# First modulation of a two-block transformer kernel computed in two column halves, with four tiles of the first chunk pair placed between the second half's products

## What is computed

```python
c_act = jax.nn.silu(c)
mod = (c_act @ w_ada[l] + b_ada[l]).reshape(B, N_SUBLAYERS, N_MOD, D_MODEL)
u = modulate(rmsnorm(h, norm1_g[l]), mod[:, 0, 0], mod[:, 0, 1])   # x * (1 + scale) + shift
h = h + FFN_RES_WEIGHT * mod[:, 0, 2][:, None, :] * swiglu(u, ffn1_w_gu[l], ffn1_w_down[l])
```

## Time and profile before

| | us |
|---|---|
| median of 3 runs | 2110.93 |
| the profiled execution | 2111.26 |
| its span | 2109.5 |
| PE busy in the span | 2085.0 (99%) |
| DVE busy | 1295.6 (61%) |
| ACT busy | 879.7 (42%) |
| POOL busy | 349.0 (17%) |

### The profile page before, as it was taken

How to read it: one execution, slowest core, us unless ns; L and a number is a source line. 1 busy time by engine, 2 the same in 40 slices (tenths; PEclk the granted TensorE clock), 3 DMA queues, 4 the chain that set the end, 5 groups by cost and what they waited for, 6 DMA issues and landing times.

```text
span 2109.5 us, 28671 instructions
## 1 busy us (share of the span) xinstructions
PE 2085.0 (99%) x9520; PEld 1711.7 (81%) x9520; DVE 1295.6 (61%) x1587; ACT 879.7 (42%) x1265; POOL 349.0 (17%) x263
## 2 busy tenths in 40 slices
PE   8999999999999999999999999999999999999998
PEld 5888888888888878888887788888888888888886
DVE  5787567678754553333357867777333577547767
ACT  5322223477543342222245656664222344334444
POOL 2999998000000200000000000022000000000000
PEclk9999999999999999999999999999999999999999
DMA  8666764322233323233323222233333233333232
GB/s 297 186 182 178 206 190 141 107 70 70 72 93 100 105 80 99 81 99 100 92 78 99 74 70 70 63 72 94 107 99 90 80 100 92 94 103 99 69 94 87
DMA packets 372645, 225.82 MB, mean 107 GB/s; under 512 B 8377, under 2 KB 361826, under 8 KB 372592
## 3 DMA queue, kind: packets, MB, share of 16 engines
q1 hardware_dynamic: 362976, 193.49, 31.4%
q0 software_dynamic: 9616, 31.64, 5.4%
HBM read 223.00 MB, written 2.10 MB: 107 GB/s over the span
## 4 chain that ended last, share of the span: by engine, by line
PE 92%; DVE 4%; ACT 2%; issue 1%; DMA 1%; SPq 1%; DVEq 0%; POOL 0%; ACTq 0%
PE ps L495 29%; PE ps L497 29%; PE ps L496 29%; PE ps L639 1%; PE ps L627 1%; PE ps L654 1%; PE ps L628 1%; PE ps L655 1%; DVE wl L1514 0%; PE ps L880 0%; DMA wada<-in_w_ada 0%; SPq L393 0%; DMA xtok<-in_x 0%; PE ps L630 0%; DVE tmp L1564 0%
## 5 line engine op out<-in xcount | busy, mean ns | idle before, releaser
L495 PE MATMUL ps<-uh,wh 128*128 128x512 f32 x1848 | 725.4, 393 | 2.0 <-DVE ul L1570 1.8
L497 PE MATMUL ps<-uh,wl 128*128 128x512 f32 x1848 | 719.9, 390 | 0.0
L496 PE MATMUL ps<-ul,wh 128*128 128x512 f32 x1848 | 719.5, 389 | 0.0
L1514 DVE TENSOR_TENSOR wl<-raw,wh 128x1024 fp32r<-128x1024 f32 x389 | 554.2, 1429 | 202.6 <-ACT wh L1024 196.1
L1024 ACT ACTIVATE wh<-raw 128x1024 fp32r<-128x1024 f32 x389 | 407.2, 1052 | 190.8 <-PE ps L497 187.7
L495 PEld LDWEIGHTS ps<-uh,wh 128*128 128x128 f32 x1848 | 347.0, 188 | 77.0 <-DVE ul L1570 3.4
L497 PEld LDWEIGHTS ps<-uh,wl 128*128 128x128 f32 x1848 | 346.8, 188 | 73.1
L496 PEld LDWEIGHTS ps<-ul,wh 128*128 128x128 f32 x1848 | 347.1, 188 | 71.0 <-issue 0.5
L495 PE MATMUL ps<-ah,wh 128*128 128x512 f32 x528 | 208.9, 396 | 0.0
L496 PE MATMUL ps<-al,wh 128*128 128x512 f32 x528 | 208.8, 396 | 0.0
L497 PE MATMUL ps<-ah,wl 128*128 128x512 f32 x528 | 208.8, 395 | 0.0
(11 more groups left out here) (337 smaller groups left out, 2389.4 us busy)
## 6 DMA issues: line engine op xcount, KB each, us to landing
raw<-in_ffn_w_gu SPq DMA_DIRECT2D x88, 512.0 KB, 4.6
raw<-in_w_in SPq DMA_DIRECT2D x57, 512.0 KB, 3.8
ada_ring<-in_w_ada POOLq DMA_DIRECT2D x56, 512.0 KB, 4.1
raw<-in_w_up SPq DMA_DIRECT2D x44, 512.0 KB, 3.8
raw<-in_w_mix_in SPq DMA_DIRECT2D x40, 512.0 KB, 3.9
raw<-in_ffn_w_down SPq DMA_DIRECT2D x32, 384.0 KB, 3.3
raw<-in_ffn_w_down SPq DMA_DIRECT2D x32, 320.0 KB, 2.9
wada<-in_w_ada SPq DMA_DIRECT2D x16, 512.0 KB, 9.8
```

Of the source, the lines that this page charges most:

```text
L495: pe.matmul(dst, lh, rh, start=first, stop=False, skip_group_check=True)
L496: pe.matmul(dst, lh, rl, start=False, stop=False, skip_group_check=True)
L497: return pe.matmul(dst, ll, rh, start=False, stop=last, skip_group_check=True)
L1514: dve.tensor_tensor(wl[:, w], raw[:, w], wh[:, w].bitcast(F32), ALU.subtract).then_inc(w_lo, 1)
```

## The change

The halves are no longer scale and shift, but the first and the last 512 features of both:

- **Loads.** `load_half(half)` issues eight DMAs of 512 KB; each takes 512 columns of the shift and the same 512 of the scale (two runs of 2 KB per row). Their semaphores and their place among SP's loads stay.
- **PE.** Within a half, PE sums all 512 scale columns and DVE all 512 shift columns. Between the second half's products come tiles 0 to 3 of the first chunk pair (after products 1, 2, 3 and 4), and tiles 4 to 7 after the second `keep_clock(2)`.
- **DVE.** `columns(half)` now ends with the gain of its four tiles. `split(0)`, `shifted_lo(0)` and `split(1)` follow the first half; then `shifted_lo` of tiles 1 to 3 alternates with the second half's sums. `normalise` of tile 3 comes before the last two sums of the first half.
- **ACT** goes tile by tile: gain, then shift; `split(1)` after tile 0 and `split(2)` ahead of tile 4.
- **POOL** normalises tiles 4 to 7, once DVE has done tiles 0 to 3.
- **att2** (DVE only). In the lead-in `split(nb + 2 + LEAD)` moves from before `first_result(3)` to after `v_lo(0)` and `maxima(0, 0)`. In the first body, `o_sum(p, 0)` and `turned_lo(p, 1)` move ahead of `split(nb + 5 + LEAD)`, so also ahead of `f_rows(p)`.
- The waits on `derived` count one more.

```diff
+            def load_half(half):
+
+                by_vector = wada[:, :].rearrange("p (v k c) -> p v k c", v=2, k=DT)
+                for k in range(DT):
+                    w = a["w_ada"][0, k * P:(k + 1) * P, 0:2 * D].rearrange("p (v c) -> p v c", v=2)
+                    sp.dma_start(by_vector[:, :, k, half * S:(half + 1) * S], w[:, :, half * S:(half + 1) * S]).then_inc(HALF_LD[half][k][0], 16)
+
+            load_half(0)
...
+            load_half(1)
...
+            def pair_tile(c, banks, k, kt, xh, xl, ready):
+
+                pe.wait_ge(ready[0], ready[1] + k + 1)
+                x = slice(k * S, (k + 1) * S)
+                for n, b in enumerate(banks):
+                    r = (c + n) % RING
+                    w = slice(r * SLOT + k * P, r * SLOT + (k + 1) * P)
+                    mm = mm3(bank(b), wh[:, w], wl[:, w], xh[:, x], xl[:, x], k == 0, k == kt - 1)
+                    if k == kt - 1:
+                        mm.then_inc(chunk_done, 1)
...
-            column_sums(1, ada_acc[1])
-
-            pe.wait_ge(h_new, 2 + 5)
+            column_sums(0)
+
+            pe.wait_ge(h_new, 2 + DT)
+            nb = AT_["ffn1"]
             for k in range(DT):
-                pe.wait_ge(*SHIFT_LD[k])
-                x = (DT + k) * D
-                mm = pe.matmul(bank(4), cbc[:, k * P:(k + 1) * P], wada[:, x:x + S], start=k == 0, stop=k == DT - 1, skip_group_check=True)
-            mm.then_inc(ada_red, 1)
+                mm = scale_sum(1, k, 4)
+                if k == DT - 1:
+                    mm.then_inc(ada_red, 1)
+                if 1 <= k <= 4:
+                    if k == 1:
+                        pe.wait_ge(w_lo, RING + nb + 2)
+                    pair_tile(nb, (0, 1), k - 1, DT, uh, ul, u_at(0))
             keep_clock(2)
 
             pe.wait_ge(ada0, 1 + 2 * DT)
-            column_sums(0, ada_acc[0])
+            pe.wait_ge(mods_done, 2)
+            column_sums(1)
             keep_clock(2)
+            for k in range(4, DT):
+                pair_tile(nb, (0, 1), k, DT, uh, ul, u_at(0))
...
+            def gained(m):
+
+                act.wait_ge(norm_t, m + 1)
+                act.wait_ge(derived, 1 if m < 4 else 2)
+                act.activation(tile(hn, m), tile(hn, m), ACT.Copy, scale=gains[:, m:m + 1]).then_inc(x_inv, 1)
+
+            def shifted_hi(m):
+
+                act.wait_ge(x_inv, 3 + m + 1)
+                act.wait_ge(mods_done, 2 if m < 4 else 4)
+                act.activation(tile(uh, m), tile(hn, m), ACT.Identity, bias=mods[:, m:m + 1]).then_inc(norm_hi, 1)
+
+            gained(0)
+            shifted_hi(0)
             split(1, 0)
...
+            for m in range(1, DT):
+                if m == 4:
+                    split(2, 0)
+                gained(m)
+                shifted_hi(m)
...
+                    if first:
+                        o_sum(p, 0)
+                        turned_lo(p, 1)
+                    if not last:
                         split(nb + 5 + LEAD, it)
...
-                    split(nb + 2 + LEAD, 0)
                     first_result(3, B_F0)
...
                 if kind == 2:
+                    split(nb + 2 + LEAD, 0)
                     normal(4)
...
+            weighted(0, range(3))
 
             dve.wait_ge(x_inv, 3)
             normalise((0, 1))
-            scale_part((3, 4, 5))
-            normalise((2,))
-            scale_part((6, 7))
+            weighted(0, (3, 4, 5))
+            normalise((2, 3))
+            weighted(0, (6, 7))
...
-            normalise((3,))
-            columns(1, 6, sq, 0)
-            dve.wait_ge(mods_done, 2)
-            gain_of(0, C_N1, 1)
-            normalise((4,))
+            columns(0, 6, sq)
             split(0, 0)
+            shifted_lo(0)
             split(1, 0)
...
+            for m in range(1, 4):
+                shifted_lo(m)
+                weighted(1, (m - 1,))
+            weighted(1, range(3, DT))
+            columns(1, 4, tmp)
+            for m in range(4, 7):
+                shifted_lo(m)
             split(2, 0)
+            shifted_lo(7)
...
+            pool.wait_ge(x_inv, 3)
+            pool.wait_ge(norm_t, 4)
+            for m in range(4, DT):
+                pool.wait_ge(h_new, 2 + m + 1)
+                pool.tensor_tensor(tile(hn, m), tile(h, m), inv[:, :], ALU.mult).then_inc(norm_t, 1)
+
             pool.wait_ge(c_act, 1)
```

More of the change, by code:

```diff
@@ L517, in dense_pair @@
                 for k in range(kt):
[L519 to L526, removed]
+                    pair_tile(c, banks, k, kt, xh, xl, ready)
                     if middle is not None and k == 3:
@@ L1407, in _ @@
             split(0, 0)
-            split(1, 0)
[L1410 to L1420, removed]
+            def gained(m):
[8 more added lines that the diff above has]
+            shifted_hi(0)
+            split(1, 0)
+            for m in range(1, DT):
[3 more added lines that the diff above has]
+                shifted_hi(m)
             ffn("ffn1", False)
@@ L1910, in body @@
                         layer_stats()
-                    o_sum(p, 0)
+                    if not first:
+                        o_sum(p, 0)
                     if kind == 2 and not last:
                         f_rows(p)
-                    turned_lo(p, 1)
+                    if not first:
+                        turned_lo(p, 1)
                     if kind == 2 and not last:
@@ L2036, in _, with weighted @@
             dve.tensor_copy(cbc[:, :].rearrange("p (k n) -> p k n", n=P), cact[:, :].unsqueeze(2).to_broadcast([P, DT, P])).then_inc(ada0, 1)
[L2038 to L2049, removed]
-                for k in ks:
[L2051 to L2057, removed]
+            def weighted(half, ks):
+                acc = ada_acc[0][:, half * S:(half + 1) * S]
+                for k in ks:
+                    dve.wait_ge(*HALF_LD[half][k])
+                    w = ada_half(0, k, half)
+                    if k == 0:
+                        dve.tensor_scalar(acc, w, cact[:, 0:1], None, ALU.mult).then_inc(ada0, 1)
+                    else:
+                        dve.wait_ge(ada0, 1 + DT * half + k)
+                        dve.scalar_tensor_tensor(acc, w, cact[:, k:k + 1], acc, ALU.mult, ALU.add).then_inc(ada0, 1)
             def normalise(ms):
@@ L2076, in columns @@
                 dve.wait_ge(ada_red, 2 * n + 2)
-                dve.tensor_tensor(mods[:, v * DT + half:(v + 1) * DT], bank(7, 400 + 4 * (1 - v), half), cols[:, c + half:c + DT],
+                dve.tensor_tensor(mods[:, n0:n0 + 4], bank(7, 400 + 4 * half, 4), cols[:, C_BADA + n0:C_BADA + n0 + 4],
                                   ALU.add).then_inc(mods_done, 1)
+                dve.wait_ge(mods_done, 2 * n + 1)
+                dve.scalar_tensor_tensor(gains[:, n0:n0 + 4], mods[:, m0:m0 + 4], 1.0, cols[:, C_N1 + n0:C_N1 + n0 + 4],
+                                         ALU.add, ALU.mult).then_inc(derived, 1)
@@ L2080, in _, with shifted_lo @@
+            def shifted_lo(m):
+                dve.wait_ge(norm_hi, m + 1)
+                dve.wait_ge(mods_done, 2 if m < 4 else 4)
+                dve.scalar_tensor_tensor(tile(ul, m), tile(hn, m), mods[:, m:m + 1], tile(uh, m).bitcast(F32), ALU.add, ALU.subtract).then_inc(u_ready, 1)
             dve.wait_ge(rms_done, 1)
             dve.reciprocal(small[:, 8:12], small[:, 4:8]).then_inc(inv_done, 1)
-            scale_part(range(3))
+            weighted(0, range(3))
             dve.wait_ge(x_inv, 3)
```

64 lines of the change are left out of this document (26 added, 38 removed).

## The result

The kernel after takes 2115.23 us (median of 20 runs, 2113.30 to 2117.45), the kernel before beside it 2112.14 (20 runs, 2110.93 to 2113.17): +3.1 us, a ratio of 1.0015 with a 95% interval from 1.0008 to 1.0021. It lies within 0.2%, on the slower side.

A forecast was written before the change was run, and what follows sets the result against it. PE, busy 99% of the span, was taken as the bound. 2111.26 (profiled execution) + 3.0 for the start − 1.4 for att2 = 2112.9, lowered 0.33 to the median: 2112.5 us, range 2109.8 to 2116.0.

The forecast's parts named there:

- Collision of POOL and DVE: Start, ahead of tile 0: POOL's ops hold DVE's two-input ops exclusively, so the gain is done at 29.8 us, not 26.3.
- Stall ahead of tile 0: First chunk pair: tile 0 starts at 33.6 us, a new PE stall of 2.3 us after product 1.
- Loads: `w_ada` loads at the start: 2 KB runs cost 5%, moving the first shift product 0.7 us to 28.6, hidden behind tile 0.
- Rival 2: PE falls to the half clock again in the new stall before tile 0: 1.9 us more, 2114.4 us; chance 20%.
- The 2.0 us between 27.87 and 36.72: Second half's products before the change: 2.0 us of PE time went to the half clock and load waits.
- Rival 4: The change gains what it aims at, with no POOL hold and no half clock in the first two products: 2108.5 us; chance 5%.
- Chain ahead of tile 4: Behind the last column sums: mods, gain, ACT's two ops and `shifted_lo` take 2.6 us, stalling PE 0.8 us past `keep_clock`.
- Sum to chunk 0: Start to the end of the first chunk pair: chunk 0 seen by ACT at 54.6 us, not 51.58, 3.0 us later.
- POOL's modulations start later, at no cost: POOL's modulation work starts some 9 us later, harmless since it ended at 367 us and PE needs it after 416.
- att2: Moved DVE ops: lead-in wait goes (−0.8 us), first body net −0.6 with 0.7 returning; in sum −1.4 (0 to −2.1).
- The 6 us of a first call on GpSimd: At the start: a first GpSimd call's code load, about 6 us, could move POOL's ops past DVE's tile 0.
- Rival 1: Start: POOL's ops come later or shorter and don't hold DVE's chain; tile 0 at 31.3, 2110.2 us; chance 20%.

The follow-up runs named there:

- the filled one with the old loads and the att2 moves: The kernel before with `keep_clock(3)` in PE's idle stretch ahead of the first shift product, plus the two att2 edits: 2110.11 us, ratio 0.9991.
- front alone: The kernel after with the two att2 edits undone, so only the new start: 2116.61 us, ratio 1.0021 against the kernel before.
- after without keep: The kernel after without the second `keep_clock(2)`, between the column sums and tile 4: 2117.08 us (7 runs), ratio 1.0026 against the kernel before.

## Why the prediction was right, and where it was wrong

No difference over 0.2% was forecast and none came (0.15%), and the time, 2112.5, lies 2.7 under the measured 2115.23. 1.2 of these come from the three runs that the forecast started from: 2110.93, where 20 runs give 2112.14. The real miss is +1.6 forecast against +3.1 measured. Point by point, in the trace:

- **Collision of POOL and DVE: right.** Gain forecast at 29.8, done at 30.2; taking POOL's ops away brings it to 27.0. That the time fits so well is partly luck: POOL's ops began at 24.19, not 22.9, behind the later inverse, took 5.77 us, not 4.8, and held mostly ops of eight and four columns, about 2.8 us in all.
- **Stall ahead of tile 0: right in place, smaller.** 1.41 instead of 2.3, since PE's products came late themselves. Tile 0 at 34.0, forecast 33.6.
- **Loads: right in rate, wrong in size, and hidden only in part.** +1.6 at the first product, not +0.7. 1.06 goes with the runs' length (the kernel before with 2 KB runs, one trace). The other 0.5 goes along with a lower rate early on, 342 GB/s from 5 to 10 us where before had 390; `x` landed later, and the first inverse came at 18.55 instead of 17.38. The kernel before with 2 KB runs doesn't show that (392 GB/s, 17.41), the filled one with the old loads and the att2 moves does (352 GB/s, 18.52), so the change isn't needed for it; what sets it stays open. PE's products ended at 32.6, still ahead of tile 0, so the wait itself was hidden. But the half clock began 2.2 us later than before (30.2 instead of 28.0) and reached into the pair's tiles.
- **Rival 2, the half clock again, came true** beside the forecast, not in its place, and this is the term that failed. From tile 0 to the end of the products the forecast had 10.7 us; it took 12.2 (34.00 to 46.17). 3.0 us of these at half clock account for 1.5. The forecast gave that 20% and reasoned from the length of the new stall alone; the clock fell earlier, behind the load gap, and did not rise again before 37.0. That the stall made it last is likely and not shown: the front alone, with a stall of 1.36 us that began after its half clock had ended, had 3.4 us of it.
- **The 2.0 us between 27.87 and 36.72: wrong as something to win.** Filling the gap removed the half clock and won nothing, because the loads bound the same products. Rival 4 rested on it.
- **Chain ahead of tile 4: right.** 0.85 us of stall against 0.8. The chain is 2.8 and not 2.6: 0.63 is the distance of ACT's ops in a row, while one op takes 0.71 in both kernels and a shift stands 0.75 behind its own gain; tile 7 is 0.27 late (0.25 forecast).
- **Sum to chunk 0:** 3.0 forecast, 5.57 measured: 0.4 at tile 0, 1.5 half clock, 0.2 at tile 4, 0.4 in the last four tiles.
- **POOL's modulations start later, at no cost: wrong.** The forecast asked when PE needs them (after 416 us), not whom they hold meanwhile. The stretch with them is 0.39 us longer in after and up to 1.42 in other kernels of the study.
- **att2: right.** −1.4 forecast, −1.32 in the trace and −1.45 in medians; 0.9 for `vtok` where 0.7 was expected.
- **The 6 us of a first call on GpSimd** (the Trainium skill, GPSIMD Engine Reference, "2.1 Instruction dispatch", which says it of a freshly loaded kernel) don't show here: four ops in 5.77 us, the first included, and the first starts right behind DVE's tile 3. Whether these ops are such a call at all isn't known. Rival 1 fell with the held ops of DVE.

## What to carry to other kernels

Work moved between products only helps where PE is idle, so first ask which stall it fills; here the same tiles, placed as cover for the chain behind the last sums (with a filler in the load gap and the normalising back on DVE), gave a kernel 6.1 us faster than the one that put them into a stretch that was full. A filler that holds the clock is worth real time only if nothing else bounds the products (of 1.7 us expected here, chunk 0 came 0.02 earlier), and where real tiles can stand, the filler can go. When work goes to GpSimd or is delayed there, price it by what stands on DVE at that moment and at the end of GpSimd's chain, however long after.

## What the runs showed of the hardware that I had not expected

- A DVE op of 128x8 that takes 0.15 us took 1.22 while GpSimd held a two-input op: the hold is by op, however small.
- The half clock behind the load gap lasted 3.4 us (before, front alone), 6.8 (before with 2 KB runs, after) or 10.2 (after without keep). It was longer in the traces in which PE stood idle for part of it (0.8, 1.4 and 2.0 us in these last three), and 3.4 us where PE worked all through it.
- Loads in runs of 2 KB moved 385 GB/s where runs of 4 KB moved 407, and the eight DMAs of the first batch took 7.86 us to issue on SP in place of 4.19 (SP's rows of after, then of before; 6.84 in the kernel before with 2 KB runs):

```profile
3.07 7.86 SPq L452 DMA_DIRECT2D wada<-in_w_ada  x8
```

```profile
3.07 4.19 SPq L444 DMA_DIRECT2D wada<-in_w_ada  x8
```
